# Two stacked blocks on one core: the delta rule's entry in another order, z read back in one transfer, k's norm inside the index logits

## The reference, cut to what matters

```python
h = rmsnorm(h_res, norm1_w)                      # block one
q, k, v, z, b, a, sc_b, sc_c, sc_x, gate_a, gate_b = split(h @ w_in)
o = gated_deltanet_bidir(q, k, v, z, b, a, ...)  # conv, silu, l2norm; delta rule both
                                                 # ways; rmsnorm per head, times silu(z)
y_a = o @ w_branch_dn
y_b = (sc_b * conv3(sc_c * sc_x)) @ w_branch_sc
h_res += (sigmoid(gate_a) * y_a + sigmoid(gate_b) * y_b) @ w_out
h_res += (silu(g) * u) @ w_down                  # gated MLP; then the final norm
q = rope(rms_norm(q)); k = rope(rms_norm(k))     # block two, sparse attention
logits = einsum('qhd,sd->qhs', rope(qi), rope(ki))
score = einsum('qh,qhs->qs', wi, relu(logits))
_, idx = top_k(where(causal, score, -inf), 128)
p = softmax(q . k[idx]); h += (p @ v[idx]) @ w_out
h += relu(norm(h) @ w1)**2 @ w2                  # then a second layer with a
                                                 # forget-gate attention and such an MLP
```

## Time and profile before

| what | value |
| --- | --- |
| median of the runs | 2771.14 us |
| the profiled execution's own time | 2775.23 us |
| its span | 2773.5 us |
| TensorE busy | 2620.6 us, 94% |
| VectorE, ScalarE, GpSimd busy | 51%, 36%, 39% |
| mean granted clock of TensorE | 0.977 |
| high half of a weight block (ScalarE, 353) | 1055 ns each |
| low half of a weight block (GpSimd, 353) | 2489 ns each |
| median time to landing of a weight block | 3.2 us |

### The profile page before, as it was taken

One profiled execution on the slowest core, in us unless ns is written; L12 is line 12 of the kernel. 1 busy time (PEld: TensorE's weight loads), 2 busy tenths in 40 slices (PEclk: granted clock), 3 DMA queues, 4 the chain that ended last, 5 costly groups with the idle time before them and its releaser, 6 DMA issues.

```text
span 2773.5 us, 47729 instructions
## 1 busy us (share of the span) xinstructions
PE 2620.6 (94%) x17707; PEld 2279.8 (82%) x17707; DVE 1407.5 (51%) x2080; ACT 988.1 (36%) x1809; POOL 1093.2 (39%) x564
## 2 busy tenths in 40 slices
PE   6998899998999999999898999999999999999998
PEld 5887798877987778887778679999999976777786
DVE  4765567614337642424778547245367234635532
ACT  4563434222222422223333763221233366422221
POOL 3333444333434444444437124444444311444443
PEclk8999999999999999999999999999999999999999
DMA  2222100123222222222211002222222200222222
GB/s 98 71 77 90 25 13 13 20 93 106 91 91 88 96 91 91 93 96 96 78 39 62 1 24 85 90 91 88 87 89 80 84 24 2 91 91 91 91 99 91
DMA packets 89092, 202.33 MB, mean 73 GB/s; under 512 B 36309, under 2 KB 38407, under 8 KB 88945
## 3 DMA queue, kind: packets, MB, share of 16 engines
q1 hardware_dynamic: 82844, 192.72, 21.5%
q10 hardware_dynamic: 6100, 7.58, 0.8%
HBM read 194.34 MB, written 5.92 MB: 72 GB/s over the span
## 4 chain that ended last, share of the span: by engine, by line
issue 55%; PE 18%; POOL 13%; DVE 6%; POOLq 3%; ACT 2%; DVEq 1%; ACTq 0%
POOL wl L514 12%; PE ps L550 8%; PE ps L1337 5%; POOLq L2466 2%; DVE work L2369 1%; DVE cout L1073 1%; DVE top L2366 1%; PE ps L1454 1%; PE ps L1453 1%; POOL xbl L2475 1%; PE ps L2122 1%; ACT dec L1592 0%; POOLq L130 0%; POOLq L2474 0%; ACT dec L1585 0%
## 5 line engine op out<-in xcount | busy, mean ns | idle before, releaser
L514 POOL TENSOR_TENSOR wl<-wraw,wh 128x1024 fp32r<-128x1024 f32 x353 | 878.4, 2489 | 1225.6 <-ACT wh L506 1225.6
L506 ACT ACTIVATE wh<-wraw 128x1024 fp32r<-128x1024 f32 x353 | 372.3, 1055 | 587.2 <-PE ps L550 481.7
L550 PE MATMUL ps<-xah,wh 128*128 128x264 f32 (+1 forms) x2672 | 505.3, 330 | 29.9 <-POOL wl L514 15.0
L550 PE MATMUL ps<-xah,wl 128*128 128x264 f32 (+1 forms) x2672 | 491.1, 324 | 0.0
L550 PE MATMUL ps<-xal,wh 128*128 128x264 f32 (+1 forms) x2672 | 487.8, 323 | 0.0
L550 PEld LDWEIGHTS ps<-xah,wh 128*128 128x128 f32 x2672 | 410.3, 191 | 83.6 <-issue 16.9
L550 PEld LDWEIGHTS ps<-xah,wl 128*128 128x128 f32 x2672 | 406.1, 190 | 41.2 <-issue 0.8
L550 PEld LDWEIGHTS ps<-xal,wh 128*128 128x128 f32 x2672 | 403.6, 189 | 40.7
L698 DVE TENSOR_TENSOR res<-res,stage 128x512 f32 (+3 forms) x112 | 81.9, 731 | 441.9 <-ACT stage L614 441.9
L550 PE MATMUL ps<-xbh,wh 128*128 128x264 f32 (+1 forms) x1392 | 273.4, 336 | 16.5 <-POOL wl L514 15.9
L550 PE MATMUL ps<-xbh,wl 128*128 128x264 f32 (+1 forms) x1392 | 270.1, 334 | 0.0
(11 more groups left out here) (378 smaller groups left out, 2949.7 us busy)
## 6 DMA issues: line engine op xcount, KB each, us to landing
wraw<-in_w SPq DMA_DIRECT2D x353, 512.0 KB, 3.2
res<-in_x SPq DMA_DIRECT2D x4, 528.0 KB, 5.6
z_out<-stage ACTq DMA_DIRECT2D x8, 256.0 KB, 2.1
res<-in_x ACTq DMA_DIRECT2D x1, 2048.0 KB, 7.9
stage<-z_out ACTq DMA_DIRECT2D x8, 256.0 KB, 2.6
out<-res SPq DMA_DIRECT2D x1, 2048.0 KB, 7.0
block_out<-yy SPq DMA_DIRECT2D x18, 56.0 KB
block_in<-mt SPq DMA_DIRECT2D x60, 8.0 KB
```

The source lines that it names most:

```text
L506: act.activation(wh[:, s * DM:(s + 1) * DM], wraw[:, s * DM:(s + 1) * DM], ACT.Copy).then_inc(hi_done, 1)
L514: pool.tensor_tensor(wl[:, s * DM:(s + 1) * DM], wraw[:, s * DM:(s + 1) * DM], wh[:, s * DM:(s + 1) * DM].bitcast(F32), ALU.subtract).then ...
L550: mm = pe.matmul(ps[:, 2 * s + h, 0:width], ws[:, s * DM + kk * P:s * DM + (kk + 1) * P], x[:, at:at + width], start=(h not in [o[0] for o ...
```

## The change

In the head ScalarE squares into eight buffers, VectorE adds them up and TensorE makes one pair of sums. The first weight's high half stands ahead of the root. The scaled tiles have a buffer each; five low halves are GpSimd's, three VectorE's, and block 0 waits for all eight. The decays are transposed after block 7 and summed after block 9. At the end of z VectorE applies head 12 ahead of the first `lower`, and ScalarE makes the exponents of the differences one block earlier. At the entry of the delta rule (step t = 0) the spread of step 1, its decay rows and differences change places with the turns of v and k and with the decayed q, and VectorE takes the q k product of step 0 ahead of `lower` of step 1. z comes back in one transfer behind the delta rule into 16 KB per partition of its own (`z_again`); the eight transfers and ScalarE's waits for them leave the gates. `act_segment` and `act_sc` lose their wait at the start; the wait of each eviction in `act_segment` is for one post more. In sparse attention the spreads for k's norm run between the second and the third pair of index heads, the turning's matmuls between the third and the fourth, in other banks; VectorE applies them between its weighted sums, ahead of the choice of keys. Cut from the diff are declarations, the functions removed (lines 844 to 892) and small shifts that are told here.

```diff
@@ -538,7 +539,7 @@
             if fresh is not None and h == 0 and n >= 2 * k:
-                pe.wait_ge(nlo, KT * fresh + kk + 3)
+                pe.wait_ge(nlo, KT * fresh + (KT + 2 if fresh == 0 else kk + 3))
             if sums is not None and h == 0 and n == k - 1:
@@ -601,8 +602,6 @@
         last = seg.b0 + seg.n == nb
-        if posts:
-            act.wait_ge(post_done, before[name] + 2)
@@ -610,7 +609,7 @@
             if posts:
-                act.wait_ge(post_done, before[name] + j + 1)
+                act.wait_ge(post_done, j + (before[name] + 2))
             act.activation(shaped(out(j, u), live), acc(b, live=live), func, **more).then_inc(acc_free, 1)
@@ -700,31 +699,28 @@
-    def norm_sum(pe, m, u):
-        pe.wait_ge(nsq, m + (KT * norms["pe"] + 1))
+    def pe_norm(pe):
+        pe.wait_ge(nused, KT - 1)
         for h in range(2):
-            mm = pe.matmul(ps[:, 4 + h, 0:HT], ones[:, :], nsqr[u][:, h * HT:(h + 1) * HT],
-                           start=m == 0, stop=m == KT - 1)
-        mm.then_inc(nused, 1)
-    def pe_norm(pe):
-        for m in range(KT):
-            norm_sum(pe, m, m % 2)
+            mm = pe.matmul(ps[:, 4 + h, 0:HT], ones[:, :], norm_sq[0][:, h * HT:(h + 1) * HT], start=True, stop=True)
         norms["pe"] += 1
-        pe.drain().then_inc(nsum, 1)
-    def norm_square(act, m, u):
-        act.wait_ge(nused, m + (KT * norms["act"] + 1))
-        act.activation(nsqr[u][:, 0:T], tile_at(res, m), ACT.Square).then_inc(nsq, 1)
+        mm.then_inc(nsum, 1)
...
                 act.wait_ge(x_in[m // 2], 16)
-            norm_square(act, m, m % 2)
+            act.activation(norm_sq[m][:, :], tile_at(res, m), ACT.Square).then_inc(nsq, 1)
         norms["act"] += 1
+        split_hi(act, Blk(0, 0))
         act.wait_ge(nsum, norms["act"])
         act.activation(two(rstd[:, :]), pair_of(4), ACT.Sqrt, bias=eps[:, 0:1], scale=1.0 / DM).then_inc(nroot, 1)
+    def dve_norm_total(dve):
+        for m in range(1, KT):
+            dve.drain()
+            dve.wait_ge(nsq, m + 1)
+            dve.tensor_tensor(norm_sq[0][:, :], norm_sq[0][:, :], norm_sq[m][:, :], ALU.add).then_inc(nused, 1)
@@ -732,7 +728,28 @@
+    LOWS_ON_DVE = 3
+    def low_part(e, m):
+        e.wait_ge(nhi, m + 1)
+        e.tensor_tensor(tile_at(xal, m), scaled[m][:, :], tile_at(xah, m).bitcast(F32), ALU.subtract
+                        ).then_inc(nlo, 1)
+    def dve_norm_apply(dve):
+        for m in range(KT):
+            dve.scalar_tensor_tensor(scaled[m][:, :], tile_at(res, m), gains[:, m:m + 1], rstd[:, :], ALU.mult,
+                                     ALU.mult).then_inc(nscaled, 1)
+        for m in range(LOWS_ON_DVE):
+            low_part(dve, m)
+    def act_norm_apply(act):
+        for m in range(KT):
+            act.wait_ge(nscaled, m + 1)
+            act.activation(tile_at(xah, m), scaled[m][:, :], ACT.Copy).then_inc(nhi, 1)
+    def pool_norm_apply(pool):
+        for m in range(LOWS_ON_DVE, KT):
+            low_part(pool, m)
...
@@ -962,9 +928,9 @@
                 sums(SUM_BLOCK[j] // 2)
-            if j == 6:
+            if j == 7:
                 pe_prep_turn(pe)
-            if j == 8:
+            if j == 9:
                 pe_prep_sums(pe)
...
@@ -1113,10 +1079,10 @@
                 apply(j - SPREAD_BLOCK)
-        for m in range(8, 12):
+        for m in range(8, 13):
             apply(m)
         next(steps)
-        for m in range(12, 16):
+        for m in range(13, 16):
             apply(m)
@@ -1487,13 +1453,15 @@
                 last_product(t - 1)
-            if t + 1 < STEPS:
+            if inner and t + 1 < STEPS:
                 each(spread_decay, t + 1)
...
                 each(turn_k, t)
+            if t == 0:
+                each(spread_decay, 1)
             if t + 1 < STEPS:
@@ -1552,11 +1520,13 @@
                 each(mask_qk, t - 1)
+            if t == 0:
+                each(decay_rows, 1)
             if t < STEPS:
                 each(masked, t - 1, 1)
-            if t + 1 < STEPS:
+            if 0 < t and t + 1 < STEPS:
                 each(decay_rows, t + 1)
@@ -1614,9 +1584,9 @@
         each(decay_diff, 0)
-        yield
         act.drain()
         each(exp_diff, 0)
+        yield
         each(exp_decay, 0)
@@ -1626,11 +1596,13 @@
                     each(product_out, t - 1, lv)
-            if t + 1 < STEPS:
+            if inner and t + 1 < STEPS:
                 each(decay_diff, t + 1)
                 each(k_tokens, t)
+            if t == 0:
+                each(decay_diff, 1)
             if t + 1 < STEPS:
@@ -1823,9 +1795,11 @@
             ahead, inner, outer = 0 < t < STEPS, 1 <= t <= STEPS, t >= 2
+            if t == 1:
+                each(decayed_qk, 0)
             if ahead:
                 each(lower, t)
-            if inner:
+            if t > 1 and inner:
                 each(decayed_qk, t - 1)
@@ -1898,10 +1872,6 @@
                 last.then_inc(hrt, 1)
-            if 9 <= j <= 12:
-                for m in (2 * j - 18, 2 * j - 17):
-                    act.wait_ge(post_done, m + 1)
-                    act.dma_start(live_stage(m % 2), z_out[m]).then_inc(z_back[m % 2], 16)
@@ -1923,8 +1893,8 @@
             dve.drain()
-            dve.wait_ge(z_back[m % 2], 16 * (m // 2 + 1))
-            g = live_stage(m % 2)
+            dve.wait_ge(z_back, 16)
+            g = z_again[:, m * SEQ:(m + 1) * SEQ]
             dve.tensor_tensor(g, g, x, ALU.mult)
@@ -1932,7 +1902,6 @@
         b0 = SEGS["sc"].b0
-        act.wait_ge(post_done, before["sc"] + 2)
         with act.Fori(0, 4) as i:
...
@@ -2106,7 +2078,21 @@
+        def k_spreads():
+            pe.wait_ge(kn_inv, 1)
+            pe.wait_ge(acc_free, b0)
+            for m in range(2):
+                for h in range(2):
+                    mm = pe.matmul(ps[:, 2 * m + h, 0:HT], spread[:, m * P:(m + 1) * P], hinv[:, h * HT:(h + 1) * HT],
+                                   start=True, stop=True)
+                mm.then_inc(kn_spread, 1)
         for m in range(4):
+            if m == 2:
+                k_spreads()
+            if m == 3:
+                rope_turn(pe, 5)
+                rope_turn(pe, 6)
             pe.wait_ge(ix_q, m + 1)
@@ -2123,15 +2109,7 @@
-        pe.wait_ge(kn_inv, 1)
-        for m in range(2):
-            pe.wait_ge(ix_act, 4 * IX - 1 + m)
-            for h in range(2):
-                mm = pe.matmul(ps[:, 4 + 2 * m + h, 0:HT], spread[:, m * P:(m + 1) * P], hinv[:, h * HT:(h + 1) * HT],
-                               start=True, stop=True)
-            mm.then_inc(kn_spread, 1)
-        rope_turn(pe, 5)
-        rope_turn(pe, 6)
+        pe.wait_ge(rope_dve, 7)
@@ -2148,8 +2126,8 @@
             if j == 1:
-                pe.wait_ge(rope_dve, 7)
                 pe.wait_ge(q_table, 1)
+                pe.wait_ge(ix_act, 4 * IX)
             if 1 <= j <= 8:
@@ -2315,13 +2293,14 @@
                                      ALU.mult, ALU.add).then_inc(ix_dve, 1)
-        for m in range(2):
-            dve.wait_ge(kn_spread, m + 1)
-            x = tile_at(pf, 8 + m)
-            dve.scalar_tensor_tensor(two(x), two(x), headgain[:, 2:3], pair_of(4 + 2 * m), ALU.mult, ALU.mult
-                                     ).then_inc(kn_app, 1)
-        rope_sine(dve, 5)
-        rope_sine(dve, 6)
+            if n in (2 * IX + 1, 2 * IX + 3):
+                m = (n - 2 * IX) // 2
+                dve.wait_ge(kn_spread, m + 1)
+                x = tile_at(pf, 8 + m)
+                dve.scalar_tensor_tensor(two(x), two(x), headgain[:, 2:3], pair_of(2 * m), ALU.mult, ALU.mult
+                                         ).then_inc(kn_app, 1)
+            if n in (3 * IX + 1, 3 * IX + 4):
+                rope_sine(dve, 5 + (n - 3 * IX) // 3)
         dve_topk(dve)
...
@@ -2998,6 +2975,10 @@
             res3 = res[:, :].rearrange("p (k t) -> p k t", t=T)
+            for u in range(2):
+                act.wait_ge(z_stored[u], 16 * 4)
+            act.dma_start(z_again[:, :].rearrange("p (k t) -> p k t", t=SEQ), z_out.rearrange("k p t -> p k t")
+                          ).then_inc(z_back, 16)
             act.dma_start(res3[:, :, NMETA:T], io["x"].rearrange("k p t -> p k t")[:, :, NMETA:T]
@@ -3038,14 +3019,13 @@
             dve.drain().then_inc(prep_dve_ones, 1)
+            dve_norm_total(dve)
             dve.wait_ge(gains_in, 16 * len(scales))
-            for i in range(4):
-                dve.wait_ge(x_in[i], 16)
             dve.tensor_tensor(gmix[:, :], gains[:, 2 * KT:3 * KT], gains[:, 3 * KT:4 * KT], ALU.mult)
             dve_norm(dve)
-            dve_norm_apply(dve, 0)
+            dve_norm_apply(dve)
             loaded(dve)
...
```

63 lines of the change are left out of this document (14 added, 49 removed).

## The result

The changed kernel takes 2727.71 us (median of four runs, 2726.84 to 2727.82) against 2772.65 for the kernel before on the same chip (2770.98 to 2774.56): a ratio of 0.9837, 95% interval 0.982 to 0.9854, 44.9 us less. Forecast were 39.2 us less. The profiled execution took 2726.84 us, with a span of 2725.1 against 2773.5.

What follows compares the result with a forecast made beforehand. TensorE, busy 94% of the span, bounds the kernel, so time comes from its idle and low-clock stretches. Terms 4 + 7.2 + 8.5 + 2.2 + 8.2 + 7.6 + 1.5 = 39.2 us take the median 2771.1 to 2732; bounds 2715 to 2749.

Steps and rivals of the forecast that it cites:

- (B): Rival: everything falls kindly, with head 8.6, entry 6, gates 10.4, segments 10; 12.8 us more saved, 2719 us; chance 0.17.
- Preparation: Preparation of the decays, one block later: TensorE's 4.63 us wait and 2.6 of slow passes go, 7.2 us saved.
- end of z: Last z blocks: the 7.26 us wait for head 12's apply and the slow pass behind it go, 8.5 us saved.
- Head: Norm of x and block 0: 4.5 us gained without the ring, 1.5 lost by a later root; 4 us taken.
- Entry: Entry of the delta rule, behind the barrier: ScalarE's exponents start 2.2 us earlier and step 1 follows, 2.2 us saved.
- Segments: ScalarE's wait at segment starts removed, the eviction's made stricter: 8.5 + 1.5 - 2.4 = 7.6 us saved.
- y_a: Segment start at 825.01: the old wait goes, but block 0 waits 2.05 us for a blocked convolution post; 1.5 us saved.
- y_b and w_out: Eviction and post become one chain of 6.08 us against a block's 5.56, delaying w_out's start: 2.4 us lost.
- Choice of keys: k's norm and turning inside the index logits: 8.7 us of tail go, logits grow 5.5 to 8.2; 1.5 us taken.
- (A): Rival: collisions of VectorE and GpSimd eat more, so 12 us less is saved, 2744 us; chance 0.23.
- (C): Rival: the stricter wait chains eviction and post in all 16 segments with posts, 67 us, 2798 us; chance 0.03.
- (D): Rival: the bound does not move, removed waits at segment starts turn into later ones; some 2766 us; chance 0.04.

## Why the prediction was right, and where it was not

The direction and the bound hold, and so does every wait that was named: each edit takes away a wait of an in-order queue ahead of TensorE. 44.9 us came where 39.2 were forecast, inside the range. That the sum lies this near is in part luck: by the traces 3.3 us were paid that no term had, 2.7 came from a loop that no edit explains, and the other terms were too low by 9.8 in total. Two of the signs failed: block 0 ended at 39.6, not at 41 to 43, and the choice of keys starts 5.2 us behind what was the last logit's end, not 7 to 8. (In rival (B) the four high ends add up to 13.0, not 12.8, which moves nothing.) The terms one by one:

- **Preparation (7.2) and end of z (8.5)**: 7.1 and 9.1 by the traces of before and after, 6.5 and 8.9 by undoing. The wait and the slow passes behind it both went. The granted clock over 85 to 99, the same blocks as the earlier trace rows, is 1.0.
- **Head (4)**: mis-sized, 5.8 (5.2 by undoing). The additions ended at 17.98 (18.7 forecast) and the root began at 20.27 (21.1). From the reciprocal's start to block 0's end it took 18.6 us where 20.7 were forecast: scalings and low halves were costed as full turns, 0.7 and 1.3, but a pair takes 1.73, and block 0's last pass takes 2.20 instead of 2.71, at a granted clock of 1.0 over the first 42 us (0.79 over the first 48 in the kernel before).
- **Entry (2.2)**: mis-sized, 4.6 and 4.4 by undoing, within its bounds of 1 to 6. The path is the forecast one, the exponents and behind them the first inverse products of step 1, but the exponents come 4.0 us earlier, not 2.2. Counted from the first operation behind the barrier they start at +6.1, where they started at +10.0 (292.21 - 282.19). The step that failed is the turns' cost: 3.7 us, read behind the wait of 4.44. With that wait gone only 1.24 us of idle time stand ahead of them, and they run in 1.9. So the spread follows at +1.9, not at +3.8:

```profile
260.24 1.08 PE L1318 MATMUL ps<-ident,qkv 128*106 128x128 f32 x8 [1.24 <-ACTq L439]
...
262.13 0.65 PE L1310 MATMUL ps<-grow,ones 48*128 48x424 f32 x2
...
266.30 2.30 ACT L1562 ACTIVATE dec<-dec,tok_b 106x106 f32<-106x106 f32 x8
```

TensorE behind the barrier in the kernel before, up to the end of spread and turns, then in the changed one, where the products behind them fit in too; the granted clock is the number behind the count:

```profile
282.19:290.05 7.86, 4.68 (x18) 0.57 0.30 102
```

```profile
260.24:266.19 5.95, 5.71 (x51) 1.00 0.39 76
```

- **Gates (8.2)**: 8.8. Heads 3 and 5 came 0.42 and 1.19 us late (0.9 and 1.3 forecast).
- **The transfer of z (0)**: here the step failed. I moved a DMA past ScalarE's queue and looked for its cost at the receiver (65 us of slack) and at the weight loads, not at the issue itself and at what stands behind it in the queue. It cost 3.3 us.
- **Segments (7.6)**: 12.8 by the traces of before and after, 11.0 (median) and 13.1 (trace) by undoing. What was to be given back came as forecast: at each of the last four starts the held-back passes run 0.32 us late (0.3 forecast), behind the blocked post below; at the first four it is 0.13 (0.1), at the gated one 1.02 (1.1). What was mis-sized is what a removed wait returns: 1.48 us at each of the last four, where I took its row, 1.2. Its row shows idle time up to the modelled end of the last matmul (0.40 us, though such matmuls start 0.23 apart), which hides 0.17 us, and the pass behind the wait was slow (2.13 instead of 2.03 us). So the last MLP gives 4.7 instead of 3.6 and the first 4.3 instead of 3.4; in the gated one the two waits of 0.45 return 0.7 each and that of 1.69 returns 1.95. The kernel before at such a start, then the changed one:

```profile
2452.28 0.40 PE L550 MATMUL ps<-xbl,wh 128*128 128x512 f32 x1
...
2453.89 2.13 PE L550 MATMUL ps<-xbh,wh 128*128 128x512 f32 x8 [1.21 <-POOL wl L514]
```

```profile
2405.05 2.35 DVE L690 TENSOR_SCALAR xbh<-stage 128x512 f32 x1 [0.19 <-issue]
...
2407.54 0.69 DVE L692 TENSOR_TENSOR xbl<-stage,xbh 128x512 f32 x1
2408.29 0.50 PE L551 MATMUL ps<-xbh,wh 128*128 128x512 f32 x1
```

- **y_a (1.5)**: 2.7; the wait that takes the old one's place is 1.83 (2.05 forecast), and behind the old wait a second pass was slow too, 2.63 us instead of 2.01, which no term had.
- **y_b and w_out (-2.4)**: -1.7. The mechanism is right to the number (a chain of 6.01 us, 6.08 forecast; the longest stall 2.08, about 2.4 forecast), the balance is not quite: the two starts returned 2.3 us (2.15 forecast), and 3.9 were lost, 1.3 in y_b's last four blocks and 2.7 in w_out's first.
- **Choice of keys (1.5)**: 1.3 up to the attention, 0.8 behind it. The size is right by two errors that cancel: the logits grew by 5.2 us, less than the 5.5 to 8.2 forecast, so 3.5 remained, and GpSimd's split at the first operation of the choice, for which no term stood, took 2.2. The 0.5 lost in the attention goes with its lower clock (0.71 against 0.75), which no term had either.

Of the rivals, (A) fell for the segments, the head and the gates, where collisions ate less than it let them, and for the entry; for the choice of keys 0.8 came, between its 0 and the forecast. (B) fell for its size: 2727.7 lies nearer to the forecast's 2732 than to its 2719. Only the segments reached what it gave them. (C) showed its mechanism only in y_b, the one post past its point of 5.4 us. (D) did not come: of the waits removed in the segments the one at y_a was followed by a new one (2.76, 1.83 now), as forecast, and the 1.69 of the gated MLP by one of 0.76.

What stays open: what the third of three issues waits for, the 2 us between trace and median for the segments, and why the loop of the delta rule gets a lower clock in one execution than in another.

## What to carry to other kernels

A DMA issue is an instruction of its engine's queue: when one is moved, look at its own duration, which grew here from 0.61 to 3.23 us or more behind two of 2 MB issued just before, and at what stands behind it; spread such issues between operations that have slack. A duration read behind a long wait is not the duration without that wait: price the operations behind a wait by rows at the clock that they will have. Where two engines take turns, as VectorE and GpSimd did here, look for an operation of the one that does not hold the other (the reciprocal here) and put the other's pass beside it; work that both could do was done sooner by the quicker one alone. For a ring of two buffers the wait for the post two back is enough where it is free of races; one post stricter makes a chain of eviction and post, harmless only while that is shorter than a block.

## What the runs showed of the hardware that was not expected

- Of three transfers issued in a row by ScalarE (2 MB, 2 MB, 64 KB) the last took 2.9 to 4.3 us to issue and the last two together 4.6 to 5.0, in eight profiles; with two in a row (2 MB, 64 KB) it was 0.40 and 0.61, and each alone takes 0.38.
- VectorE's reciprocal (3.45 us) and GpSimd's split (2.34 us) run side by side without loss; seven two-operand additions beside the same split take 7.48 instead of 5.52 us.
- A scaling and a low half that alternate between VectorE and GpSimd take 1.73 us the pair. Alone on VectorE a scaling takes 0.69 (5.52 / 8) and a low half 0.63 (5.03 / 8), so both there take 1.32.
- The turns, 3.7 us behind an idle stretch of 4.4 us (granted clock 0.57 from the barrier to their end), took 1.9 behind one of 1.2 (granted clock 1.0).
- A stretch of 2320 matmuls in one and the same order took 255.0 us at a mean granted clock of 0.98, and 263.5 at 0.93.
